# FoX stage of a hybrid streaming encoder: the causal mask added on VectorE instead of TensorE, and its units taken in the reverse order

## The reference, cut to what matters

```python
    cum = jnp.cumsum(logf, axis=1).transpose(0, 2, 1)
...
        sc = jnp.einsum('bqhd,bkhd->bhqk', qi, k, preferred_element_type=jnp.float32) * SCALE
        sc = sc + ci[..., :, None] - cum[:, :, None, :]
        qpos = i * Q_BLOCK + jnp.arange(Q_BLOCK)
        sc = jnp.where(kpos[None, :] <= qpos[:, None], sc, -jnp.inf)
        p = jax.nn.softmax(sc, axis=-1)
        return jnp.einsum('bhqk,bkhd->bqhd', p.astype(v.dtype), v)
```

## Time and profile before

| | us |
|---|---|
| median of 3 runs (1514.61 to 1515.33) | 1515.33 |
| the profiled execution | 1514.46 |
| its span, first to last instruction | 1512.7 |
| PE busy in the span | 1489.5 |
| DVE busy | 994.9 |
| ACT busy | 609.8 |
| POOL busy | 648.6 |

### The profile page before, as it was taken

How to read it: one execution, slowest core, us unless ns; L and a number is a source line. 1 busy time by engine, 2 the same in 40 slices (tenths; PEclk the granted TensorE clock), 3 DMA queues, 4 the chain that set the end, 5 groups by cost and what they waited for, 6 DMA issues and landing times.

```text
span 1512.7 us, 25850 instructions
## 1 busy us (share of the span) xinstructions
PE 1489.5 (98%) x9807; PEld 1396.5 (92%) x9807; DVE 994.9 (66%) x1915; ACT 609.8 (40%) x1265; POOL 648.6 (43%) x554
## 2 busy tenths in 40 slices
PE   7999999999999999999999999999999999999996
PEld 6999999999998999999888999999999998778885
DVE  7876656666665376865546987555555556478986
ACT  5143534434343256755332343333223333444463
POOL 5833333333332312244222678888778780000104
PEclk9999999999999999999999999999999999999999
DMA  6132232122133611268331122222222229633668
GB/s 190 59 103 81 72 105 87 39 76 67 33 119 124 229 52 38 67 197 266 98 115 32 42 86 90 81 78 65 85 85 86 85 66 324 200 95 108 191 186 157
DMA packets 156477, 164.89 MB, mean 109 GB/s; under 512 B 14006, under 2 KB 122042, under 8 KB 156355
## 3 DMA queue, kind: packets, MB, share of 16 engines
q1 hardware_dynamic: 124441, 114.08, 24.4%
q10 hardware_dynamic: 30090, 45.89, 9.0%
q0 software_dynamic: 1824, 3.28, 1.6%
HBM read 125.04 MB, written 39.85 MB: 109 GB/s over the span
## 4 chain that ended last, share of the span: by engine, by line
PE 87%; DVE 7%; POOL 1%; ACT 1%; DMA 1%; issue 1%; ACTq 0%; SPq 0%; POOLq 0%; DVEq 0%
PE bank L1230 18%; PE bank L1232 18%; PE bank L1231 18%; PE bank L1238 6%; PE bank L1236 6%; PE bank L1237 6%; PE bank L1265 4%; PE bank L1385 2%; PE bank L1356 1%; PE bank L1355 1%; PE bank L1746 1%; PE bank L1748 1%; DVE conv L2995 1%; DMA ysr<-d_y 1%; PE bank L1508 0%
## 5 line engine op out<-in xcount | busy, mean ns | idle before, releaser
L1230 PE MATMUL bank<-ht_h,ring_h 128*128 128x352 f32 x816 | 268.9, 330 | 0.6 <-POOL ring_l L1068 0.6
L1232 PE MATMUL bank<-ht_h,ring_l 128*128 128x352 f32 x816 | 262.7, 322 | 0.0
L1231 PE MATMUL bank<-ht_l,ring_h 128*128 128x352 f32 x816 | 261.9, 321 | 0.0
L1230 PE MATMUL bank<-m_h,ring_h 128*128 128x264 f32 x648 | 184.2, 284 | 1.3 <-DVE m_l L3038 1.2
L1231 PE MATMUL bank<-m_l,ring_h 128*128 128x264 f32 x648 | 184.2, 284 | 0.0
L1232 PE MATMUL bank<-m_h,ring_l 128*128 128x264 f32 x648 | 183.9, 284 | 0.0
L1004 POOL TENSOR_TENSOR ring_h<-raw,att 128x256 fp32r<-128x256 f32 x100 | 68.3, 713 | 244.5 <-PE bank L1232 229.5
L1230 PEld LDWEIGHTS bank<-ht_h,ring_h 128*128 128x128 f32 x816 | 153.2, 188 | 3.6 <-issue 0.9
L1231 PEld LDWEIGHTS bank<-ht_l,ring_h 128*128 128x128 f32 x816 | 153.9, 189 | 0.7
L1232 PEld LDWEIGHTS bank<-ht_h,ring_l 128*128 128x128 f32 x816 | 153.3, 188 | 0.0
L1230 PE MATMUL bank<-tb_h,ring_h 128*128 128x264 f32 x456 | 129.9, 285 | 0.0
(11 more groups left out here) (394 smaller groups left out, 3950.1 us busy)
## 6 DMA issues: line engine op xcount, KB each, us to landing
raw<-in_w_up SPq DMA_DIRECT2D x44, 512.0 KB, 3.9
raw<-in_w_in SPq DMA_DIRECT2D x34, 512.0 KB, 3.9
rb<-in_w_down SPq DMA_DIRECT2D x66, 256.0 KB, 2.9
d_y<-conv SPq DMA_DIRECT2D x22, 529.0 KB, 3.6
d_gate<-gst ACTq DMA_DIRECT2D x48, 176.0 KB, 1.9
a<-d_y SPq DMA_DIRECT2D x33, 256.0 KB, 5.6
ra<-d_y SPq DMA_DIRECT2D x33, 256.0 KB, 2.9
gm<-d_gate ACTq DMA_DIRECT2D x8, 528.0 KB, 4.3
```

The source lines that it names most:

```text
L1230: nc.tensor.matmul(out, wh, xh, start=start, stop=False, skip_group_check=onto)
L1231: nc.tensor.matmul(out, wh, xl, start=False, stop=False, skip_group_check=onto)
L1232: return nc.tensor.matmul(out, wl, xh, start=False, stop=stop, skip_group_check=onto)
```

## The change

The mask matmuls, `maskr` and `idr` go. Instead `mask_unit(u)` adds the mask on DVE to the 128 columns of the decays that unit `u` meets on its diagonal, in place. That needs the units of a head from wide to narrow, since a wider unit reads those columns without the mask. `mask_unit(s + 1)` stands behind the negated maximum of unit `s`, `mask_unit(s)` in front of a head's first unit.

The step without a filler is now the last of the third and fourth pair; `K_ROWS` and `V_ROWS` move there from 9 and 11 to 7 and 10. At the second step of all, the first half of the filler stands in front of `scores`. `head_keys` copies first the half of the rows that DVE reads, and signals behind it. An exponential of one element stands ahead of the first unit on ACT. The cached keys of the sample frames are loaded in three pieces instead of one, two of them during the second head of the last pair.

```diff
-UNITS = [(h, b, r) for h in range(2) for b in range(4) for r in range(2)]
+UNITS = [(h, b, r) for h in range(2) for b in reversed(range(4)) for r in reversed(range(2))]
...
-        elif s in (-1, 2) or s > NU + 2:
+        elif s in (-1, NU - 1) or s > NU + 2:
             return []
         else:
-            i = s if s < 2 else s - 1
+            i = s if s < NU - 1 else s - 1
...
-    K_ROWS, V_ROWS, FIRST_V = [7, 9, 9, 9], [9, 11, 11, 11], 1
+    K_ROWS, V_ROWS, FIRST_V = [7, 9, 7, 7], [9, 11, 10, 10], 1
...
-                    last = i == len(halves(b, r)) - 1
                     nc.tensor.matmul(out[:, 0:w], q, kh[:, h, o:o + w], start=True, stop=False)
-                    mm = nc.tensor.matmul(out[:, 0:w], q, kl[:, h, o:o + w], start=False, stop=not last)
-                    if last:
-
-                        mm = nc.tensor.matmul(out[:, w - P:w], idr[:, :], maskr[:, 0:P],
-                                              start=False, stop=True)
-                    mm.then_inc(s_full, 1)
+                    nc.tensor.matmul(out[:, 0:w], q, kl[:, h, o:o + w], start=False, stop=True).then_inc(s_full, 1)
...
+                    if g == FIRST_V:
+                        (n, c), = fillers(p, s)
+                        dense_chunk(n, c, part=range(KT // 2))
...
+            def past_keys(t0, t1, units):
+
+                act.wait_ge(s_free, LAST * PIECES + BEFORE[units])
+                act.dma_start(past[:, t0:t1, :], cache_fox_k[0, 0].rearrange("(t r) h d -> r t (h d)", r=P)[:, t0:t1, :]
+                              ).then_inc(smp_keys, 16)
...
+                half = (h + turn) % 2
...
-                if half:
+                if half == h:
                     ins.then_inc(khi, 1)
...
+            nc.scalar.activation(att[0:1, 59:60], zero[0:1, :], ACT.Exp)
...
+            def mask_unit(u):
+
+                h, b, r = UNITS[u]
+                block = negc[:, h, SPAN * b + P * r:SPAN * b + P * r + P]
+                order.mark(V.tensor_tensor(block, block, cst[:, P:2 * P], ALU.add))
...
+                        if s % HEAD_U == 0 and g:
+                            mask_unit(s)
+                        order.catch_up()
...
+                        if (s + 1) % HEAD_U:
+                            mask_unit(s + 1)
```

More of the change, by code:

```diff
@@ L153, in program @@
     cst, o_cst = place("cst", [P, CONST_W])
-    maskr, _ = place("maskr", [P, P], F32R)
-    idr, _ = place("idr", [P, P], F32R)
     stat, _ = place("stat", [P, 64])
@@ L1375, in values @@
                     pe.wait_ge(v_ready, 2 * p + h + 1)
-                pe.wait_ge(t_free, at_unit[2 * v + 1] + len(halves(b, 1)))
+                pe.wait_ge(t_free, at_unit[2 * v + 1] + len(halves(*UNITS[2 * j + 1][1:])))
                 wait(pe, pv_free, v)
@@ L1418, in _ @@
                         src = ktn if s == K_ROWS[p] else vqn
-                        dense_chunk(n, c, part=range(KT // 2))
+                        if g != FIRST_V:
+                            dense_chunk(n, c, part=range(KT // 2))
                         if s == K_ROWS[p]:
@@ L1436, in _ @@
             n = SLAB["gate", 10]
-            pe.wait_ge(smp_keys, 16 * 2)
+            pe.wait_ge(smp_keys, 16 * 4)
             for p in range(PAIRS):
@@ L1892, in decay_load, with head_keys @@
                               ).then_inc(negc_in, 16)
-            def head_keys(p, h, half):
+            def head_keys(p, h, turn):
+                half = (h + turn) % 2
                 act.wait_ge(freed_dve, reads["dve"][slab_end(KEYS[p])])
@@ L1989, in _ @@
                     if s == NU:
-                        act.wait_ge(s_free, S_FOX)
-                        past_load(smp_keys, cache_fox_k)
+                        past_keys(2, 3, NU)
+                    if p == LAST and s == HEAD_U + 2:
+                        past_keys(0, 2, HEAD_U)
+                    if p == LAST and s == HEAD_U + 5:
+                        past_keys(3, 4, HEAD_U + 4)
                     if s == NU or s == NU + 1:
@@ L2499, in _ @@
             dve.wait_ge(setup_in, SETUP)
-            V.tensor_copy(maskr[:, :], cst[:, P:2 * P])
-            dve.wait_ge(ident_in, 16)
-            V.tensor_copy(idr[:, :], ident)
             dve.wait_ge(misc_pe, MP_CACHE)
@@ L2599, in _ @@
             dve.wait_ge(negc_in, 32)
+            mask_unit(0)
             for p in range(PAIRS):
```

## The result

| | before | after |
|---|---|---|
| median, us | 1514.77 (20 runs, 1512.21 to 1517.82) | 1517.16 (20 runs, 1515.11 to 1519.86) |
| profiled execution, us | 1514.46 | 1517.21 |
| its span, us | 1512.7 | 1515.4 |

The ratio of after to before is 1.0017, with a 95% interval of 1.0011 to 1.0023. The kernel became slower by 2.4 us, where 1.2 us less was forecast. The spans of the two profiled executions differ by 2.7 us.

A forecast was written before the change was run, and what follows sets the result against it. The prediction took PE to bound the kernel. Mask matmuls -7.2, last steps +2.8, row transposes +1.7 and start +1.5 gave -1.2 us, from the median 1515.3 to 1514.1 us, range 1510.8 to 1517.5.

The forecast's parts named there:

- What follows is PE-bound as well, so a shift of FoX reaches the end: Behind FoX: PE also bounds what comes next, so FoX's forecast change of -1.2 us arrives in the total.
- The rest at nothing: Keys in three pieces, `head_keys` signalling one copy earlier and earlier fillers were all taken to cost PE nothing.
- the upper end: Range limit 1517.5 us: each mask matmul gains only 0.06 us, 3.8 us in all instead of 7.2.
- The second rival: DVE falls behind among wide units, its additions and key subtractions slowed beside POOL (GpSimd); slower, 1518.9 us, chance 0.12.
- mask matmuls: PE in FoX: dropping 64 mask matmuls gains 0.112 us each by distance between starts, 7.2 us.
- last steps, third and fourth pair: No filler there: PE waits 1.3 us ahead of `values` in both pairs, plus 0.2 for queries; 2.8 us.
- row transposes: At `V_ROWS` and behind second filler halves PE waits for DVE's `lows`, less one wait at `K_ROWS`; 1.7 us.
- start: First units of FoX, now wide: PE waits for DVE's copies and later `lows`; 1.5 us lost.
- The addition: One 128x128 mask addition on DVE, estimated at 0.28 us, 18 us for all 64, mostly hidden behind fillers.
- The 0.7 in the fourth step: Start of FoX: `lows` of unit 1 come 0.7 us late for the transposes, DVE carrying key subtractions up to 1.70.
- The wait ahead of the first `values`: Start of FoX: an existing PE wait of 0.4 us that the new delay covers, subtracted from the start's cost.

The follow-up runs named there:

- Run 1: Changed kernel with ACT's eight loads of the sample decays issued one step later, behind the last head_queries; 1512.86 us, ratio 0.9992 to the kernel before.
- run 6: Changed kernel with only DVE's order altered: the subtraction for the sample queries moved behind the copies of the cached keys; 1512.59 us, ratio 0.9988 to before.
- run 4: Kernel before without the 64 mask matmuls and nothing in their place, so not causal inside a block; 1508.63 us, ratio 0.9964 to before.
- run 7: Changed kernel without the 64 mask additions on DVE, so not causal inside a block; 1516.13 us, ratio 1.0013 to the kernel before.
- run 3: Changed kernel with the step without a filler at 14 instead of 15 in the third and fourth pair; 1515.63 us, ratio 1.0010 to before.
- r2_keys_one_piece: Changed kernel with the cached keys loaded in one piece after FoX instead of three; 1517.46 us, ratio 1.0020 to the kernel before.

## Why the prediction was wrong

**The step that failed** is "What follows is PE-bound as well, so a shift of FoX reaches the end", and with it "The rest at nothing". The text followed PE up to the last unit and asked there only what the step without a filler costs. It did not ask what the last `values` of all had covered. With the narrow units last, that cover fell from 1.7 to 0.3 us, GpSimd's split moved forward by 1.6 into DVE's subtraction, and the sample section cost +5.1 us. Runs 1 and 6 show it: with either edit the section is back at 11.3 and 11.4, and the times of 1512.86 and 1512.59 are on the side that was forecast. So the direction was missed for a place that the sum left out, not for a term inside it. That 1517.16 lies within the stated 1510.8 to 1517.5 all the same is luck: the upper end stood for a mask matmul worth 0.06 us, and run 4 shows 0.10.

Run 1's ratio reaches to 1.0001, so its own gain over before is not certain; run 6's interval lies below 1.

The second rival's mechanism, DVE held up by GpSimd, was at work, but cost little where it was expected. The rows of the 64 additions in after, first ns (least, median, most), then busy us and mean ns:

```profile
L2598 DVE TENSOR_TENSOR negc<-negc,cst x64: 277/282/712, 77.0 to 425.5; 128x128 f32<-128x128 f32 x64
...
L2598 DVE TENSOR_TENSOR negc<-negc,cst 128x128 f32<-128x128 f32 x64 | 22.8, 357 | 0.0
```

The mean lies well above the median. 45 of them took 0.28 or 0.29 us; 41 of these met no GpSimd instruction, and 3 more began 0.07 us ahead of one. The other 19 took 0.31 to 0.71 us, and each of them began while a GpSimd instruction was running. One of the 19:

```profile
273.74 0.61 POOL L1002 TENSOR_TENSOR ring_h<-raw,att 128x256 fp32r<-128x256 f32 x1
...
273.81 0.68 DVE L2598 TENSOR_TENSOR negc<-negc,cst 128x128 f32<-128x128 f32 x1
```

Together the 64 took 22.8 us where 18.0 would be 0.282 each. Of these 4.8 us PE saw little, since a filler stands behind most of them: all additions together cost PE 0.8 us (run 7). What cost was one subtraction at the end, with no slack behind it.

**Inside FoX** the forecast was -1.2 and the trace has -1.5. Term by term:

| term | forecast | measured |
|---|---|---|
| mask matmuls | -7.2 | -6.6 (run 4) |
| last steps, third and fourth pair | +2.8 | +2.6 |
| row transposes | +1.7 | +1.5 |
| start | +1.5 | +0.6 |
| sum | -1.2 | -1.9, in the windows -1.5 |

- *The mask matmuls*: the distance of 0.112 us each is confirmed (run 4), and 14 us of busy time was the wrong measure. Run 4's FoX gives 0.6 less than the product. About 0.1 of that is idle time of PE, which rose from 0.15 to 0.25 us in the window; the rest I did not place. The 81 ns of the Trainium skill (TensorE: Matmul & The Clock Gate, section Back-to-back issue gap) would give 5.2 us, further from 6.6 than the row's 7.2.
- *The addition* took 0.282 us by its median against the estimate of 0.28, and 0.357 by its mean. Run 7 has the 18 us of busy time that were forecast for all of them (18.7). DVE's busy time rose by only 15 from before to after because the rest of its work took 3.8 less.
- *The last steps*: in the row that follows, `values` starts 1.35 us after two transposes that take some 0.25, so 1.1 us late; 1.3 was forecast, 0.15 of it for a signal that takes 0.06 here (`lows` end at 342.28). The 0.25 is an estimate: in run 3, where a filler stands in front of them, the same two take 0.35, by which the term would be 2.4 and not 2.6. At the third pair's end PE starts the next scores 0.3 late and the matmul behind them 0.4 (0.2 forecast). Run 3 gives 1.5 us of it back.

```profile
340.99 0.40 PE L1263 MATMUL bank<-cst,ssb 128*128 128x128 f32 x2
...
342.34 0.39 PE L1373 MATMUL bank<-pt_h,vhl 128*128 128x256 f32 x1 [0.94 <-DVE pt_l L2452]
...
343.20 0.33 PE L1378 MATMUL bank<-pt_l,vhl 128*128 128x256 f32 x1
...
343.68 0.50 PE L1352 MATMUL bank<-kh,qsw 128*128 128x512 f32 x1 [0.15 <-DVE qsw L2577]
```

- *The row transposes*: 0.3, 0.4 and 0.4 us ahead of them in the second to fourth pair (0.4, 0.6, 0.6 forecast), and 0.1 each in five places behind the second half of the filler; less the 0.12 that went at the first pair's `K_ROWS`.
- *The start*: the waits ahead of the sample row transposes and of unit 0's came, 0.4 and 0.6 us (0.7 and 0.5 forecast). The 0.7 in the fourth step did not: the first key subtraction took 1.22 us, not the 1.70 that I had read from the earlier trace rows. The wait ahead of the first `values` went as forecast.

```profile
84.52 0.32 PE L1230 MATMUL bank<-ht_h,ring_l 128*128 128x352 f32 x1
85.10 0.28 PE L1263 MATMUL bank<-cst,vqn 128*32 128x128 f32 x1 [0.25 <-DVE rowsn L2548]
85.79 0.63 PE L1263 MATMUL bank<-cst,ssb 128*128 128x128 f32 x4 [0.40 <-DVE rowsn L2548]
```

The sum of the measured terms is 0.4 us more gain than the windows show, or 0.6 with the lower value for the last steps. That remainder stays open.

What also stays open is how much of the 2.7 us wait for `ktc` is the collision with GpSimd. The subtraction's excess is 2.48 - 1.22 = 1.26 us; no run removed that alone. Nor did a run remove the slower clock alone: its 2.6 us is what is left of the 5.1, and runs 3 and 7, with the same wait, had sections of 15.3 us, so that this part ranges from 1.4 to 2.6 us. And it is open why one of the eight issues took 0.87 to 1.44 us in each of the five profiles that have them at the end of the new order (after and runs 2, 3, 6 and 7), and none over 0.48 in the others.

## What to carry to other kernels

When the order of wide and narrow pieces is turned round, list what the last wide piece of the stage covered on every other engine (issues of DMAs among them), and follow the engines past the end of the stage up to the next place where the bounding engine waits for them. A wait on that engine of two or three us can cost more than itself, since TensorE may run at half its clock behind it (1.4 to 2.6 us on top of 2.5 here); removing any one link of the chain that made it may be enough. Matmuls are priced by the distance between starts: that, and not their busy time, gave the gain to within 0.6 of 7.2 us.

## What the runs showed of the hardware

- The granted clock fell to 0.50 inside a PE wait of 2.7 us in after and stayed there until 454.0, 6 us after PE had resumed. In r3_free_step_14, with a wait as long, it fell only 0.5 us after PE had resumed and was back at about 449.3, 3.4 us later. In the two waits of about 1 us ahead of `values` in after it stayed 1.00.
- Eight DMA issues hold ACT for 4.7 us, one of them for 1.33 us and most for 0.45, with no wait in the trace; before, the same eight took 3.8 us.
- A DVE operation with two SBUF inputs that begins while GpSimd's instruction on the weights runs is held up, however short: 19 of 64 additions took 0.31 to 0.71 us for 0.28. Whether the two meet is a matter of tenths of a us. The same subtraction took 1.22 us before and in r1_issues_later, 2.48 in after and in r3_free_step_14, 2.62 in r2_keys_one_piece and 2.95 in r7_no_mask_adds.
